# Moving the prompt attention of a hybrid decoder layer in among its gate projections, with keys stored sorted by residue

## The reference, cut to what matters

```python
def residues(t):
    return t.reshape(B, n_sub, dilation, H, dh).transpose(0, 2, 1, 3, 4).reshape(Z, n_sub, H, dh)
...
s = jnp.einsum('znqhd,znkhd->znhqk', qb.astype(F32), kb.astype(F32)) * (dh ** -0.5)
mx = jnp.max(s, axis=-1, keepdims=True)
e = jnp.exp(s - mx)
den = jnp.sum(e, axis=-1, keepdims=True)
o = jnp.einsum('znqhk,znkhd->znqhd', e / den, vb.astype(F32))
```

## Time and profile before

| | |
|---|---|
| median of 3 runs | 2912.58 us (2911.98 to 2912.82) |
| the profiled execution | 2907.64 us |
| its span | 2905.4 us, mean granted clock 0.957 |
| TensorE busy | 2757.0 us (95%) |
| VectorE, ScalarE, GpSimd busy | 1002.9, 412.8, 815.1 us |
| DMA | 222.05 MB, mean 76 GB/s |

### The profile page before, as it was taken

The page is one execution under the profiler, slowest core; times in us unless marked ns, Lnnn a source line. Parts: engine busy times, 40 slices in busy tenths (PEclk is TensorE's granted clock), DMA queues, the critical chain, the costliest instruction groups (busy, mean ns, idle before and its releaser), DMA issues. The chain is left out here.

```text
span 2905.4 us, 39691 instructions
## 1 busy us (share of the span) xinstructions
PE 2757.0 (95%) x16354; PEld 2630.5 (91%) x16354; DVE 1002.9 (35%) x2040; ACT 412.8 (14%) x847; POOL 815.1 (28%) x202
## 2 busy tenths in 40 slices
PE   7999999999979999999979988888899999999997
PEld 6999999999979999999967774378899999999997
DVE  5222222222481101330036654553742222222226
ACT  4000000000120010001123331111210000000002
POOL 3333333333233233333200001204233333333330
PEclk9999999999999999999978877889999999999999
DMA  4111111111124222223163234553011111111101
GB/s 151 44 44 43 43 43 43 43 43 44 43 73 150 86 90 88 93 77 119 47 188 101 83 107 167 221 159 124 30 44 44 43 43 43 43 43 43 43 15 62
DMA packets 86246, 222.05 MB, mean 76 GB/s; under 512 B 10532, under 2 KB 64220, under 8 KB 71164
## 3 DMA queue, kind: packets, MB, share of 16 engines
q1 hardware_dynamic: 61512, 191.02, 19.2%
q10 hardware_dynamic: 24628, 29.50, 2.9%
HBM read 174.61 MB, written 45.89 MB: 76 GB/s over the span
## 5 line engine op out<-in xcount | busy, mean ns | idle before, releaser
L732 PE MATMUL ps<-h_hi,whi 128*128 128x384 f32 (+1 forms) x3072 | 1010.0, 329 | 18.8 <-DVE h_lo L1597 11.9
L734 PE MATMUL ps<-h_hi,wlo 128*128 128x384 f32 (+1 forms) x3072 | 1007.4, 328 | 0.0
L733 PE MATMUL ps<-h_lo,whi 128*128 128x384 f32 (+1 forms) x3072 | 1007.1, 328 | 0.0
L648 POOL TENSOR_TENSOR whi<-raw,con 128x2048 fp32r<-128x2048 f32 x98 | 353.4, 3606 | 2014.3 <-PEq L716 1437.6
L732 PEld LDWEIGHTS ps<-h_hi,whi 128*128 128x128 f32 x3072 | 578.7, 188 | 17.7 <-issue 10.5
L733 PEld LDWEIGHTS ps<-h_lo,whi 128*128 128x128 f32 x3072 | 578.6, 188 | 5.5 <-issue 5.1
L734 PEld LDWEIGHTS ps<-h_hi,wlo 128*128 128x128 f32 x3072 | 578.5, 188 | 0.0
L650 POOL TENSOR_TENSOR wlo<-raw,whi 128x2048 fp32r<-128x2048 f32 x98 | 453.2, 4624 | 7.7
L685 PE MATMUL ps<-act_hi,whi 128*128 128x384 f32 (+1 forms) x1056 | 346.0, 328 | 9.8 <-DVE x L1617 7.8
L1617 DVE SCALAR_TENSOR_TENSOR x<-ps,x 128x384 f32<-128x384 f32 (+1 forms) x528 | 281.9, 535 | 200.8 <-PE ps L687 199.2
L687 PE MATMUL ps<-act_hi,wlo 128*128 128x384 f32 (+1 forms) x1056 | 345.5, 327 | 0.0
(11 more groups left out here) (216 smaller groups left out, 2430.6 us busy)
## 6 DMA issues: line engine op xcount, KB each, us to landing
raw<-stream SPq DMA_DIRECT2D x99, 1024.0 KB, 4.8
vc<-vc_in SPq DMA_DIRECT2D x8, 1170.0 KB, 6.7
kc<-kc_in SPq DMA_DIRECT2D x8, 1152.0 KB, 9.8
zgate<-stage ACTq DMA_DIRECT2D x16, 384.0 KB, 2.5
sgate<-zgate SPq DMA_DIRECT2D x16, 384.0 KB, 3.3
zqko<-stage ACTq DMA_DIRECT2D x12, 384.0 KB, 2.5
oc<-o_att SPq DMA_DIRECT2D x8, 396.0 KB, 6.5
va_out<-sva ACTq DMA_DIRECT2D x24, 130.0 KB, 1.8
```

What stands on the lines that cost most here:

```text
L648: pool.tensor_tensor(hi, raw[:, j, :], con[:, C_ONES:C_ONES + 1].to_broadcast([P, SLAB]), ALU.mult).then_inc(hi_split, 1)
L732: pe.matmul(out, w_hi, h_hi[:, k, a:a + w], start=(k == 0), stop=False)
L733: pe.matmul(out, w_hi, h_lo[:, k, a:a + w], start=False, stop=False)
L734: mm = pe.matmul(out, w_lo, h_hi[:, k, a:a + w], start=False, stop=(k == KT - 1))
```

## The change

The attention leaves the mixed stretch. The 24 gate tiles are cut in halves of four input pieces each, which makes 48 slots. Slot n holds half a tile and, from slot 20 on, `att_scores(n-20)`, `att_turn(n-21)`, `att_values(n-22)`. After slot 47 nine more slots have attention alone (units 28 to 34 are scored there). Only then the recurrence runs, without attention. ScalarE has the same slots, with `gate_unit` at the end of each tile; VectorE runs all maxima and outputs in one loop and `args(0)` after it. SP loads keys and values of groups 0 and 1 near the start of the gates, stores outputs 0 to 25, waits for the end of the gates, loads head 0, and stores the other outputs.

The other parts:

- Queries and keys of groups 1 and 2 are stored sorted by residue (modulo 4 and 8): the rope passes read PSUM and the tables with that step and write `stage` in order, split where a chunk holds sample columns; the store of a tile becomes one transfer per half, in pieces of 96 or 48 columns, and one more for the sample columns. The host puts the keys back in order.
- Heads lie in pairs on partitions 0 to 63 and 64 to 127 (`aqk`), each of the two writes a bank of its own, and each bank has its own mask matmul. The two banks are 4 and 5, and from unit 28 on alternately 0 and 1.
- The outputs of the recurrence alternate between banks 2 and 7.
- Memory is laid out anew: attention in and around the place of `x`, the odd heads of the recurrence in place of the slabs.

```diff
+def nd_bank(w):
+    return (2, 7)[w % 2]
...
+SLOTS = 48
+FIRST_SLOT = 20
+def score_banks(u):
+    return 0 if u >= SLOTS - FIRST_SLOT and u % 2 else 4
...
 SP
+            sp.wait_ge(x_saved, 48)
+            sp.wait_ge(h_ready, 48)
+            sp.wait_ge(v_stored[0], 16 * 23)
+            sp.wait_ge(stored[0], stored_before(36, 0))
+            sp.wait_ge(stored[1], stored_before(36, 1))
+            sp.wait_ge(v_stored[1], 16 * 22)
+            for g in range(2):
+                load_keys(g)
+                load_values(g)
+            for s in range(3 * LOOPED, S_UP):
+                slab_behind(s, s % 3)
+            before_end = SLOTS - FIRST_SLOT - 2
+            for u in range(before_end):
+                store_outputs(u)
+            sp.wait_ge(up_full, PU_UP)
...
             load_head(0)
-            load_values(0)
             load_late(0)
-            behind = (lambda: load_keys(1), lambda: load_values(1), lambda: load_head(1))
-            for u in range(LEAD):
+            for u in range(before_end, NU):
                 store_outputs(u)
-                behind[u]()
+            load_head(1)
             load_late(1)
...
 PE, outputs
-                num, dn = ps[:, 2, 0:n], ps[:, 2, P:P + n]
+                b = nd_bank(w)
+                num, dn = ps[:, b, 0:n], ps[:, b, P:P + n]
                 pe.wait_ge(pm_ready, w + 1)
-                if w >= 1:
-                    pe.wait_ge(hn_ready, w)
+                if w == 1:
+                    pe.wait_ge(o_ready, NU)
+                if w >= 2:
+                    pe.wait_ge(hn_ready, w - 1)
...
 PE, att_scores
-                pe.matmul(ps[:, b, :], idb[:], mask.unsqueeze(1).to_broadcast([P, nh, nk * P]), start=True, stop=False)
-                for i in range(nh):
-                    q = tokens(aq[:, s, h0 + i, :], g, blk)
-                    k = tokens(ak[:, s, h0 + i, :], g, blk - (nk - 1), nk)
-                    mm = pe.matmul(ps[:, b, i * nk * P:(i + 1) * nk * P], q, k, start=False, stop=(i == nh - 1))
+                for r in range(2):
+                    pe.matmul(ps[:, b + r, 0:256], idb[:], mask.unsqueeze(1).to_broadcast([P, nh // 2, nk * P]), start=True, stop=False)
+                for i in range(nh // 2):
+                    j = h0 // 2 + i
+                    for r in range(2):
+                        q = tokens(aqk[64 * r:64 * r + 64, s, 0, j, :], g, blk)
+                        k = tokens(aqk[64 * r:64 * r + 64, s, 1, j, :], g, blk - (nk - 1), nk)
+                        mm = pe.matmul(ps[:, b + r, i * nk * P:(i + 1) * nk * P], q, k, start=False, stop=(i == nh // 2 - 1))
...
 PE, the slots
+            def attention_slot(n):
+                u = n - FIRST_SLOT
+                if 0 <= u < NU:
+                    att_scores(u)
+                if 0 <= u - 1 < NU:
+                    att_turn(u - 1)
+                if 0 <= u - 2 < NU:
+                    att_values(u - 2)
+            for n in range(SLOTS):
+                q, late = divmod(n, 2)
...
+                pair_unit(j % 3, c, PU_F + 36 + q, q % 2, ks=range(4 * late, 4 * late + 4))
...
+                attention_slot(n)
+            for n in range(SLOTS, FIRST_SLOT + NU + 2):
+                attention_slot(n)
...
 ACT, the store of a rope tile
-                    store(u, dst[:, :, a:a + w].rearrange("s p t -> p s t"))
+                    if r == 1:
+                        store(u, dst[:, :, a:a + w].rearrange("s p t -> p s t"))
+                    else:
+                        wp = min(w, SEQ - a)
+                        for half in range(2):
+                            act.dma_start(dst[half, :, 0:SEQ].rearrange("p (r q) -> p r q", r=r)[:, :, a // r:(a + wp) // r],
+                                          stage[:, u % 2, half, 0:wp].rearrange("p (r q) -> p r q", r=r)).then_inc(stored[u % 2], 16)
...
 DVE
+            for n in range(NU + 2):
+                if n < NU:
+                    att_max(n)
+                if n >= 2:
+                    att_out(n - 2)
             dve.wait_ge(mix_const, 16 * 4)
             args(0)
```

More of the change, by code:

```diff
@@ L92, in attention_units, with head_of, key_stores, stored_before @@
     return out
+def head_of(nh, i):
+    return i if nh == 2 else 2 * (i % 2) + i // 2
 UNITS = attention_units()
+DILATION = (1, 4, 8)
+def key_stores(u):
+    if not 18 <= u < 36:
+        return 1
+    j, c = divmod(u - 18, NC)
+    return 1 if j % 3 == 0 else 2 + (c == NC - 1)
+def stored_before(u, par):
+    return 16 * sum(key_stores(v) for v in range(par, u, 2))
 NU = len(UNITS)
@@ L716, in release, with pair_unit @@
                 pe.sem_inc(slab_free, 1)
-            def pair_unit(j, c, unit, par, h_before=None, sum_at=None):
+            def pair_unit(j, c, unit, par, h_before=None, sum_at=None, ks=range(KT)):
                 a, w = CHUNKS[c]
-                pe.wait_ge(pair_free, unit + 1)
-                for k in range(KT):
+                if ks[0] == 0:
+                    pe.wait_ge(pair_free, unit + 1)
+                for k in ks:
                     if h_before is not None:
@@ L845, in _ @@
                             h_hi[:, k, a:a + w], h_lo[:, k, a:a + w]), KT).then_inc(acc_full, 1)
-            with pe.Fori(0, 3) as i:
+            with pe.Fori(0, 2) as i:
                 for j in range(6):
@@ L939, in norm_head @@
                 pe.wait_ge(sqh_ready, h + 1)
-                if h < H - 1:
-                    pe.wait_ge(kw_ready, 9 * (h + 1) + c + 3)
-                else:
+                if h == 0:
                     pe.wait_ge(p_ready, NU)
                     pe.wait_ge(pt_ready, NU)
-                pe.matmul(bank(sums_bank(h, c), w), ones, ss[:, a:a + w], start=True, stop=True).then_inc(ss_full, 1)
+                else:
+                    pe.wait_ge(rs_read, 3 * (h - 1) + c + 1)
+                pe.matmul(bank(4 + c, w), ones, ss[:, a:a + w], start=True, stop=True).then_inc(ss_full, 1)
             def tokens(t, g, blk, n=1):
@@ L998, in att_values @@
                 mm.then_inc(ov_full, 1)
-            att_scores(0)
-            for u in range(LEAD):
-                att_scores(u + 1)
-                att_turn(u)
-                if u == 0:
-                    scores(0)
-                att_values(u)
+            def attention_slot(n):
[6 more added lines that the diff above has]
+                    att_values(u - 2)
@@ L1397, in _, with att_exps @@
-            gate_unit(0, 1, 1)
-            gate_unit(0, 1, 2)
-            with act.Fori(1, 4) as i:
-                for j in range(2):
-                    for c in range(NC):
-                        gate_unit(i, j, c)
+            def att_exps(u):
+                g, blk, h0, nh, nk = UNITS[u]
+                act.wait_ge(mx_full, u + 1)
+                if u >= 2:
+                    act.wait_ge(pt_full, u - 1)
+                wd = nk * P
+                b = score_banks(u)
+                for i in range(nh):
+                    r, n = divmod(i, nh // 2)
+                    ins = act.activation(ap_[:, u % 2, i * wd:(i + 1) * wd], ps[:, b + r, n * wd:(n + 1) * wd], ACT.Exp,
+                                         bias=amx[:, u % 4, i:i + 1])
+                ins.then_inc(p_ready, 1)
```

275 lines of the change are left out of this document (134 added, 141 removed).

## The result

The changed kernel takes 2887.53 us (median of 4 runs, 2886.93 to 2890.14) against 2912.70 for the kernel before (4 runs, 2911.98 to 2914.25): a ratio of 0.992, with a 95% interval of 0.9905 to 0.9935. The forecast was 2915, an even trade. It is faster by 25 us, inside the range and close to the 2884 of rival (b), but not what I called likeliest. The profiled execution took 2886.93 us with a span of 2884.8.

The account below looks back on a forecast made before the run. TensorE was taken as the bound, at least 90% busy almost everywhere, with low clock in the mixer. Removing 292.9 us and adding 70 + 35 + 190.6 = 295.6 gave span 2908, median about 2915; range 2886 to 2940.

Parts of the forecast that it names:

- an even trade: Whole kernel, likeliest case: parts within about 10 us, 2904 to 2924 us; chance 0.45.
- rival (b): Recurrence mostly at full clock (162 to 175 us), head pairs overlap (62 to 66): 2884, less firmly to 2903; chance 0.32.
- Part 1: Attention among the gates: 28 scores, 27 turns and 26 values add 70 us, ends 62 and 78.
- I take a quarter: Scores of paired heads among the gates: overlap taken as a quarter, giving 70 us; full overlap would save 12 us.
- Part 2: Attention tail behind the gates: nine slots, with about 8 us standing for a store, 35 us, ends 30 and 40.
- Part 3: The recurrence alone, without attention: 190.6 us; about 162 if warm, 200 with everything low.
- I take 2.75: Recurrence steps with two output banks, between 2.30 us at full and 2.92 at low clock: 32 x 2.75 = 88 us.
- rival (e): Recurrence: the second output bank brings nothing, steps stay 3.9 us, 37 us more, so 2952; chance 0.03.
- Part 4: Rope and its stores: 6.4 us instead of 2.5 per tile, cost nothing, up to 40 us if over 18.

Follow-up runs that it names:

- Halves in turn: The changed kernel with mask and scores of the lower 64 rows first, then those of the upper 64: 2914.64 us.
- paired and sorted kernel: The kernel before with paired head halves and sorted queries and keys, attention still beside the recurrence: 2879.06 us.
- all behind: The changed kernel with all 35 units of attention behind the gates, none among them: 2899.5 us.
- unrolled kernel: The changed kernel with TensorE's loop over the rope projections written out: 2874.62 us.

## Why the prediction was wrong, point by point

**Part 1, the step that failed first.** "I take a quarter" for the pairing, 70 us. It measured 62.3, the end with full overlap (62), and that end is what the trace of the slot shows: 0.63 us for 1.06. Halves in turn shows it by undoing it, +19.5 us in the same stretch. The Trainium skill, TensorEngine Tiling (Array Packing), section Key Properties, was right with the half that I weighed less: different tiles work in parallel. Its other half, the drain at a change of mode, shows here as 0.1 us per half at most. The trace of before had no instruction on the upper rows; nothing in it spoke for the quarter that I took, and the end with full overlap deserved at least the same weight. ScalarE's cover held: 93.3 of 245.1 us busy, no wait of TensorE among the gates over 0.5 us for it.

**Part 2** said 35 us with a stall of 8 for a store. It was 38.8 by another road. SP issued the head's loads in 7 us, not 10.3, and the wait for the store was 0.36 us. What stood instead were one late exponential of 2.5 us (the last sigmoids and a table load were ahead of it) and then slots of 4.2 us at 0.50, as between these two masks:

```profile
1538.53 0.63 PE L995 MATMUL ps<-amb,idb 128*128 128x256 bf16 x2
1542.76 0.63 PE L995 MATMUL ps<-amb,idb 128*128 128x256 bf16 x2
```

The sum was near only by luck: a wait of 8 us that did not come and slots that were longer than assumed cancelled.

**Part 3, the larger miss.** 190.6 us forecast, 177.3 measured. The step that failed is "I take 2.75": it took the low clock for nearly all steps. In the trace the clock is at full level in the runs of steps between the breaks of a head (1585 to 1595, 1625 to 1630, 1670 to 1675, 1710 to 1715), and there the hidden states are 2.30 us apart, VectorE's own cycle as the earlier trace rows gave it:

```profile
1585.46 0.95 DVE L1959 RECIPROCAL den<-den 128x128 f32<-128x128 f32 x1
1587.75 0.95 DVE L1959 RECIPROCAL den<-den 128x128 f32<-128x128 f32 x1
1590.04 0.95 DVE L1959 RECIPROCAL den<-den 128x128 f32<-128x128 f32 x1
```

Of the 35 distances between neighbouring reciprocals 16 are 2.2 to 2.5 us and six are 2.8 to 3.3; the others span the breaks. The low clock sits in the sample steps (0.50 from 1600 to 1620, for one) and in steps near the breaks. By heads I had 51.6, 45.5, 45.5 and 40.3 us, and it was 48.5, 43.8, 43.9 and 37.2. Nearly all of the rest are 4 us of norm sums that cost nothing of their own. That the second bank matters is shown by the run with one bank: +22.7, less than the 37 that I had for it (rival (e)).

**Part 4** was right at no cost, and wrong in its numbers. A tile's stores were to take 6.4 us at 50 ns a packet. Queue of ScalarE's stores between 1190 and 1285 us, before and after:

```profile
q10 hardware_dynamic: 3264, 4.46, 12.7%
```

```profile
q10 hardware_dynamic: 17280, 4.46, 21.1%
```

12.7% and 21.1% of 16 engines for 95 us are 193 and 321 us. A third of the bytes (group 0) is stored as before; the other two thirds cost 129 us before and 256 after, in some 16,200 packets of 16 ns. That is a factor of 2.0 for the same bytes, and the price per packet that I took from larger packets was three times too high. The Trainium skill, DMA: Bandwidth & Descriptors, table Specifications, puts a read-modify-write on pieces under 512 B; the trace agrees with the doubling that I had drawn from it and doesn't show the mechanism. Two of the six rope passes of a sorted tile of 384 columns took 0.83 to 0.99 us for 0.56, hidden.

**What I didn't see at all.** TensorE's loop holds 18 projection tiles a turn. Before, it turned three times and held most of the gates too; in the change it turns twice, since the gates are written out as slots. The idle time on "issue" between 1000 and 1290 us is 5.8 us before and 2.8 after, some 2 to 3 us a turn. Writing the loop out gains 9.1 us beside the recurrence. In the changed kernel it gains 6.4 by the first sigmoid and 8 to 13 in all, 6 of them in a tail that the edit doesn't touch.

**The sum.** -7.7 (gates) + 3.8 (tail) - 13.3 (recurrence) - 3.3 (start) - 2.6 (rest) - 4.3 (the profiled execution's place beside its median) = -27.4, from 2915 to 2887.6. So the larger half of the miss was the size of a step and of the pairing, both toward rival (b). Of (b) the overlap of the pairs came out (62.3, in its 62 to 66). Its recurrence mostly at full clock did not: it took 177.3 us at a mean clock of 0.69, outside its 162 to 175, and the tail 38.8 for 32. That its 2884 is so near is in part luck: its own sum with the measured parts is 2912.6 - 292.9 + 62.3 + 38.8 + 177.3 = 2898, and 10 us of start, rest and place of the median, which no part of the forecast held, make up the difference.

**And a question that I didn't ask.** I priced the change as one trade. The runs with one thing at a time show effects of opposite sign. Cheaper scores are worth 34 us by the medians (31 by the ratio) with attention left where it was. The move without the second output bank gives all of it back (one bank: 2906.59, ratio 0.9993), and the second bank, which the move makes free, returns about 20 (22.7 in the recurrence). What is left is a loss of 11 us against the paired and sorted kernel (2890.5 for 2879.06), although the move has one turn of TensorE's loop fewer. The tail at the low clock, 38 us of attention where a wait of 15 us stood, is a part of the bill but not shown to be its cause: with all units among the gates there is no tail, and the time is no better. An estimate by the marks: a unit costs 2.3 us among the gates. Beside the recurrence it costs (448.8 - 183.0 - 15 - 176.4) / 35 = 2.1, if the recurrence is priced as with two banks, and 1.5 with the 199.1 of one bank, which is what it had there. So the place among the gates isn't cheaper.

## What to carry to other kernels

Where a change makes work cheaper and also moves it, price the two apart, and build the cheap half without the move: here it alone gave more than the whole. Work moved into a stretch that is full costs its full time (here 62.3 us for 28 units); look first for a wait to fill (here 15 us of loads and 6 us of arguments). Where two engines take turns, count the step at the pace of the slower one at full clock first, and read from the trace in which pieces the clock is low before giving all steps that price.

## What was not expected of the hardware

- Two fp32 matmuls of 64 rows on different halves of the rows overlapped fully: four in 0.63 us alternating, two in 0.63 us on the same half.
- The clock did not follow how busy TensorE was in one stretch: in "all behind" it was busy 17.66 of 20 us at 0.50 and 19.89 of 20 at 1.00. In the changed kernel it was busy 23.64 of 24 us at 0.51 in the tail (1536 to 1560), and only 6.21 of 10 at 1.00 between 1585 and 1595. The tail of the unrolled kernel ran at 0.84, the same code in the changed one at 0.63; the cause is open.
- Strided reads cost less once paired: score work fell by 16.6 us for sorting alone, but only by 9.8 (37.8 to 28.0) once paired.
- A packet of 128 to 384 bytes (184 on average) took 16 ns of a DMA engine, one of about 1.4 KB 59 ns: per byte twice as long.
